# Two attention turns among the last gating slabs, tanh in the gate, first exponents in score banks, casts of the head norms in the second head

## What is computed

```python
p = softmax(q k^T)                       # 4 heads, 2 components each
a = p[:, :, 0] - lam * p[:, :, 1]
da = rmsnorm(a @ v, da_subln_w) * (1 - lam_init)
...
log_g = log_sigmoid(z @ w2 + b) / 16     # forward and backward gates
go = gla_bidirectional(gq / 8, gk, gv, log_g_f, log_g_b)
go = rmsnorm(go, gla_norm_w) * silu(gr)
h = h + concat([da, go]) @ w_out
```

## Time and profile before

| | us |
|---|---|
| median of 3 runs | 2437.65 |
| lowest, highest | 2434.55, 2437.88 |
| profiled execution | 2438.38 |
| its span in the profile | 2436.6 |
| granted TensorE clock, mean over the span | 0.984 |

### The profile page before, as it was taken

How to read it: one execution, slowest core, us unless ns; L and a number is a source line. 1 busy time by engine, 2 the same in 40 slices (tenths; PEclk the granted TensorE clock), 3 DMA queues, 4 the chain that set the end, 5 groups by cost and what they waited for, 6 DMA issues and landing times.

```text
span 2436.6 us, 38068 instructions
## 1 busy us (share of the span) xinstructions
PE 2334.8 (96%) x13568; PEld 1298.9 (53%) x13568; DVE 1700.0 (70%) x2984; ACT 1053.1 (43%) x1496; POOL 535.7 (22%) x418
## 2 busy tenths in 40 slices
PE   7999899999999998899999999988999989999998
PEld 3446774555555566655555555563444444443454
DVE  5326775578899989978888888868353447776235
ACT  4265442666666654543333333344422233332233
POOL 0001001567788631124222222104000010000001
PEclk9998999999999999999999999999999999999998
DMA  5200012487899669899999999913233323332321
GB/s 179 78 27 1 1 57 92 144 287 289 302 324 343 226 228 331 326 336 361 377 363 361 363 356 362 343 53 113 78 113 100 100 87 96 103 97 96 100 86 52
DMA packets 164871, 470.79 MB, mean 193 GB/s; under 512 B 17616, under 2 KB 70736, under 8 KB 163984
## 3 DMA queue, kind: packets, MB, share of 16 engines
q1 hardware_dynamic: 109312, 289.59, 34.9%
q0 software_dynamic: 36864, 134.23, 14.8%
q10 hardware_dynamic: 18576, 45.36, 4.9%
HBM read 421.67 MB, written 47.45 MB: 193 GB/s over the span
## 4 chain that ended last, share of the span: by engine, by line
PE 82%; DVE 12%; issue 2%; ACT 2%; DMA 1%; POOL 1%; DVEq 0%; SPq 0%; ACTq 0%; POOLq 0%
PE psum L536 25%; PE psum L537 24%; PE psum L538 24%; DVE arena L2043 2%; PE psum L426 1%; DVE arena L510 1%; DVE arena L2081 1%; DVE arena L2078 1%; DVE arena L2082 1%; PE psum L990 1%; PE psum L876 1%; PE psum L962 1%; DMA arena<-in_urows,arena 1%; PE psum L850 0%; DVE arena L2079 0%
## 5 line engine op out<-in xcount | busy, mean ns | idle before, releaser
L536 PE MATMUL psum<-arena 128*128 128x384 f16 (+2 forms) x3648 | 1261.3, 347 | 35.1 <-DVE arena L467 13.2
L537 PE MATMUL psum<-arena 128*128 128x384 f16 (+2 forms) x3648 | 1264.5, 347 | 0.0
L538 PE MATMUL psum<-arena 128*128 128x384 f16 (+2 forms) x3648 | 1257.7, 346 | 0.0
L536 PEld LDWEIGHTS psum<-arena 128*128 128x128 f16 x3648 | 354.2, 97 | 367.1 <-issue 51.2
L538 PEld LDWEIGHTS psum<-arena 128*128 128x128 f16 x3648 | 353.9, 97 | 324.0 <-issue 8.1
L537 PEld LDWEIGHTS psum<-arena 128*128 128x128 f16 x3648 | 353.6, 97 | 311.8 <-issue 8.1
L510 DVE SCALAR_TENSOR_TENSOR arena<-arena 128x1024 f16<-128x1024 f32 x216 | 268.2, 1244 | 297.6 <-ACT arena L497 297.1
L497 ACT ACTIVATE arena<-arena 128x1024 f16<-128x1024 f32 x216 | 226.1, 1050 | 255.9 <-PE psum L538 243.8
L1622 ACT ACTIVATE arena<-arena 128x1024 f16<-128x1024 f32 x128 | 135.3, 1057 | 299.8 <-PE psum L538 285.8
L516 POOL TENSOR_TENSOR arena<-arena 128x1024 f16<-128x1024 f32 x104 | 214.4, 2061 | 105.4 <-ACT arena L505 104.4
L438 POOL TENSOR_TENSOR arena<-arena 128x512 f32<-128x512 f32 x15 | 19.8, 1321 | 918.4 <-ACT arena L393 918.4
(11 more groups left out here) (251 smaller groups left out, 2179.7 us busy)
## 6 DMA issues: line engine op xcount, KB each, us to landing
arena<-in_w SPq DMA_DIRECT2D x320, 512.0 KB, 3.6
arena<-in_v SPq DMA_DIRECT2D x128, 512.0 KB, 6.0
early_activations<-arena ACTq DMA_DIRECT2D x124, 192.0 KB, 5.1
arena<-early_activations SPq DMA_DIRECT2D x124, 192.0 KB, 5.9
gate_matrix<-arena ACTq DMA_DIRECT2D x5, 4096.0 KB, 16.1
arena<-gate_matrix SPq DMA_DIRECT2D x32, 640.0 KB, 8.0
arena<-in_xT SPq DMA_DIRECT2D x4, 512.0 KB, 6.0
arena<-in_urows,arena POOLq DMA_INDIRECT x128, 6.9
```

Source lines behind the costliest of these rows:

```text
L536: nc.tensor.matmul(ps, a_h, b_h, start=first, stop=False)
L537: nc.tensor.matmul(ps, a_h, b_l, start=False, stop=False)
L538: return nc.tensor.matmul(ps, a_l, b_h, start=False, stop=last)
```

## The change

**Gating and the first two turns.** PE's scores of turn 0 stand between the second and the third gating slab, those of turn 1 between the third and the fourth. ACT's exponentials and DVE's maxima and differences of these turns follow the gate of the second and third slab in the same way. The first transposes wait for three gates, and the first mixing of values for the fourth. The gate is tanh(x/2) + 1 times x; its factor 1/2 and the slabs' scale are put into the recurrence's norm.

**Exponents 0 and 1** of the recurrence go to banks 1 and 3 instead of 6 and 7. Those of step 0 stand on PE ahead of turn 15's transposes, those of step 1 ahead of its values; ACT's exponentials move with them. The waits for the last transposes' copies and the last head's output pass to exponents 2 and 3. DVE's product of the meta keys moves behind the first level.

**Head norms.** In the first head DVE only scales; a new semaphore `head_scaled` releases the wide level. The casts and subtractions stand at the ends of the first eight steps of the second head.

```diff
         def expo(n, rows=P):
-            return psum[0:rows, (6 + n % 2) * 512:(7 + n % 2) * 512]
+            b = 6 + n % 2 if n >= 2 else 1 + 2 * n
+            return psum[0:rows, b * 512:(b + 1) * 512]
...
-            for n in range(N_GR, N_WO):
-                pe.wait_ge(gate_out, 1 + (n - N_GR + 1))
-                chunk(pe, n, slot(n), bank(4 + n - N_GR))
...
                 if turn == 0:
-                    pe.wait_ge(silu_out, HEADS)
+                    pe.wait_ge(silu_out, HEADS - 1)
...
             def mix_values(turn):
                 h, t = divmod(turn, TT)
                 pe.wait_ge(turn_out, turn + 1)
+                if turn == 0:
+                    pe.wait_ge(silu_out, HEADS)
...
-            pe.wait_ge(proj_out, 4)
-            for turn in range(HEADS * TT):
+            for n in range(N_GR, N_WO):
+                pe.wait_ge(gate_out, 1 + (n - N_GR + 1))
+                chunk(pe, n, slot(n), bank(4 + n - N_GR))
+                if n == N_GR + 1:
+                    pe.wait_ge(proj_out, 4)
+                    scores(0)
+                elif n == N_GR + 2:
+                    scores(1)
+            for turn in range(2, HEADS * TT):
                 scores(turn)
...
                 if n >= 2:
                     pe.wait_ge(e_exp, n - 1)
+                if n == 2:
+                    pe.wait_ge(turn_out, HEADS * TT)
+                elif n == 3:
+                    pe.wait_ge(av_out, HEADS)
...
                 if h == 0:
-                    pe.wait_ge(mixl_out, 1)
+                    pe.wait_ge(head_scaled, HEADS)
...
-                nc.scalar.activation(sgr[:, n - N_GR, :], bank(4 + n - N_GR), ACT.Sigmoid, scale=ISW).then_inc(sig_out, 1)
+                nc.scalar.activation(sgr[:, n - N_GR, :], bank(4 + n - N_GR), ACT.Tanh, scale=ISW / 2).then_inc(sig_out, 1)
+                if 1 <= n - N_GR <= 2:
+                    turn_exp(n - N_GR - 1)
...
+                nc.vector.scalar_tensor_tensor(out=sgr[:, n - N_GR, :], in0=sgr[:, n - N_GR, :], scalar=1.0,
+                                               in1=bank(4 + n - N_GR), op0=ALU.add,
+                                               op1=ALU.mult).then_inc(silu_out, 1)
+                if 1 <= n - N_GR <= 2:
+                    scores_max(n - N_GR - 1)
+                    difference(n - N_GR - 1)
...
+                scaled = nc.vector.scalar_tensor_tensor(out=o, in0=o, scalar=w, in1=bank(h),
+                                                        op0=ALU.mult, op1=ALU.mult)
+                if k == 0:
+                    scaled.then_inc(head_scaled, 1)
+                    return
+                dchain.link(scaled)
+                dchain.link(nc.vector.scalar_tensor_tensor(out=o, in0=o, scalar=ISW / 2, in1=sgr[:, h, :],
                                                            op0=ALU.mult, op1=ALU.mult))
-                if k:
-                    dchain.link(nc.vector.tensor_tensor(o, o, sgr[:, h, :], ALU.mult))
...
+            def head_cut(h, low):
+                o = otmp[:, h, :]
+                if not low:
+                    dve.wait_ge(head_scaled, h + 1)
+                    dchain.link(nc.vector.tensor_copy(xh[:, h, 0:T], o))
+                else:
+                    last = nc.vector.tensor_tensor(xl[:, h, 0:T], o, xh[:, h, 0:T], ALU.subtract)
+                    if h == HEADS - 1:
+                        last.then_inc(mixl_out, 1)
...
+                    if h == 1 and p < 2 * HEADS:
+                        head_cut(p // 2, p % 2)
```

More of the change, by code:

```diff
@@ L917, in _ @@
             pe.wait_ge(gate_cut, 1 + TT)
+            exponents(0)
+            turn_over(HEADS * TT - 1)
+            mix_values(HEADS * TT - 2)
             for h in range(HEADS):
@@ L1399, in _, with turn_exp @@
             last.then_inc(proj_out, 1)
+            def turn_exp(turn):
+                for c in range(2):
+                    u = 2 * turn + c
+                    act.wait_ge(max_done, u + 1)
+                    if turn >= 2:
+                        act.wait_ge(diff_done, turn - 1)
+                    nc.scalar.activation(pr[:, u % 4, :], psum[:, (2 * c + 1) * 512 - TM // 2:(2 * c + 1) * 512 + TM // 2], ACT.Exp,
+                                         bias=nmx[:, u % 4:u % 4 + 1],
+                                         accum_out=zs[:, u % 4:u % 4 + 1]).then_inc(exp_done, 1)
             cuts.upto(N_WO - 1)
@@ L1455, in step_exp @@
                                      scale=1.0 / (16 * GS)).then_inc(e_exp, 1)
+            turn_copy(HEADS * TT - 2)
             step_exp(0)
+            turn_copy(HEADS * TT - 1)
+            act.wait_ge(em_in, 1)
+            nc.scalar.activation(Emm[0:DH, :], bank(2, HEADS * M)[0:DH], ACT.Exp,
+                                 scale=1.0 / (16 * GS)).then_inc(em_exp, 1)
+            step_exp(1)
+            head_out(HEADS - 1)
             def head_squares(k, sqs, heads=range(HEADS)):
@@ L1847, in _ @@
             cuts.upto(N_WO - 1)
-            for n in range(N_GR, N_WO):
-                dve.wait_ge(sig_out, n - N_GR + 1)
-                nc.vector.scalar_tensor_tensor(out=sgr[:, n - N_GR, :], in0=bank(4 + n - N_GR), scalar=ISW,
-                                               in1=sgr[:, n - N_GR, :], op0=ALU.mult,
-                                               op1=ALU.mult).then_inc(silu_out, 1)
             def decayed(h, li):
```

58 lines of the change are left out of this document (20 added, 38 removed).

## The result

| | before | after |
|---|---|---|
| median of 4 runs, us | 2437.69 | 2421.30 |
| lowest, highest | 2434.55, 2437.88 | 2419.86, 2424.14 |
| profiled execution | 2438.38 | 2424.14 |
| its granted TensorE clock, mean | 0.984 | 0.989 |

Measured twice more, six runs each, the same kernel gave medians of 2425.39 and 2424.47; over all sixteen runs the median is 2424.1 (2419.86 to 2432.32), 13.4 us under 2437.5, the median of all 56 runs of the kernel before. The direction and the steps were right. What was wrong is the size of some terms, and how far one kernel's executions lie apart.

What follows compares the result with a forecast made beforehand. PE, busy for 96% of the span, was taken to bound the kernel. The terms 8.0 + 1.5 + 3.2 + 1.6 - 2.2 - 0.2 = 11.9 us gave 2425.8 us, range 2422.5 to 2432.5.

Steps and rivals of the forecast that it cites:

- part 1: Turns 0 and 1 between the gating slabs: turn 1's values mixed at 200.8 instead of 208.80, gain 8.0 us.
- part 2: Passage into the recurrence: first exponents in score banks remove PE's waits of 0.40 and 0.89 us, gain 1.5 us.
- part 3: Recurrence's first head: casts and subtractions moved out bring the wide level 3 x 1.07 = 3.2 us forward.
- the wide level at full clock: End of the recurrence's first head: PE's waits shrink and the clock stays at 2.4 GHz, another 1.6 us.
- casts in the second head: Recurrence's second head: moved casts and subtractions exceed DVE's idle time, loss 2.2 us, bounds 0 and 4.3.
- product with a scalar: Recurrence's norms: a product with a scalar replaces a plain one, 0.77 against 0.69 us, four times, loss 0.2 us.
- Rival D: Scores between slabs wait for a late key copy or exponential, and the slabs with them; 2428.5 us, chance 0.08.
- The sentence on the tanh: Gating slabs: tanh shares the exponentials' table and so allows the interleaving; the removed load by itself worth 0 to 0.1 us.
- All later stages only start earlier: Stages behind the edited stretch: assumed only to start earlier, with no further term added to the 11.9 us.
- A: Behind the slabs the clock falls again, holding back up to 6.8 us; gain 5.1, time 2432.5, chance 0.20.
- B: Ahead of the first head's wide level the clock still falls; gain 10.3, time 2427.4, chance 0.14.
- Rival C: Attention behind the slabs: half clock lasts over 24 us and the kernel is slower, 2441.8 at 32 us; chance 0.03.

Runs made afterwards that it cites:

- the version with the casts elsewhere: Changed kernel with the casts and subtractions four at a time in DVE's waits at the second step of the second and third heads; 2426.12 us, ratio 0.9949.
- the turns alone: Kernel before with only turns 0 and 1 between the gating slabs and the tanh gate; 2431.86 us, ratio 0.9984.
- the filling in the kernel before: Kernel before with ten matmuls that nobody reads in PE's two waits behind the slabs; 2433.64 us, ratio 0.9979.

## Why the prediction was right or wrong

All sizes below are from the first profile of after against that of before. PE stood 0.27 us earlier already at the gating slabs, ahead of anything the change touches, which is the start in the table; the lead at 400 us is 13.4 us.

| step | forecast, us | trace, us |
|---|---|---|
| start | 0 | 0.3 |
| part 1, turns among the slabs | 8.0 | 7.9 |
| part 2, exponents in score banks | 1.5 | 1.95 |
| part 3, up to the wide level | 3.2 | 3.6 |
| the wide level at full clock | 1.6 | 1.7 |
| casts in the second head | -2.2 | -2.0 |
| product with a scalar | -0.2 | 0.0 |
| sum | 11.9 | 13.4 |

**Part 1 was right, row by row.** Turn 2's scores at 192.65 (forecast 192.9), turn 3's 2.92 us later (2.9), turn 1's mixing 7.99 us after the slabs' end (7.9). Rival D did not occur: there is no idle time ahead of the third and fourth slab. Its timeline of DVE shows what was not foreseen, one line that took four times its usual time; the slab hid it, since the exponential after it was needed only behind the slabs:

```profile
186.10 2.12 DVE L1887 TENSOR_SCALAR arena<-arena 128x528 f32<-128x528 f32 x1
...
192.18 0.50 DVE L1887 TENSOR_SCALAR arena<-arena 128x528 f32<-128x528 f32 x1
```

**The sentence on the tanh was wrong.** "But it is what allows the interleaving" rested on no row. The right working would have been ACT's budget in a slab: 5.2 us against 0.6 for the gate, 1.4 for two exponentials and 2.6 for two loads. The tanh itself takes as long as the sigmoid, 1.09 us for two:

```profile
180.34 1.28 ACT L1421 ACT_TABLE_LOAD   x1
181.63 1.09 ACT L1421 ACTIVATE arena<-psum 128x512 f32<-128x512 f32 x2
184.20 0.70 ACT L1414 ACTIVATE arena<-psum,arena 128x528 f32<-128x528 f32 x1 [1.48 <-DVE arena L1877]
```

**Part 2 was 0.45 us too small.** The mis-sized term is PE's own work, which I had put at nothing. From the mixing of turn 1 to the first level before, the window is

```profile
208.80:258.97 50.17, 47.46 (x342) 36.27 (x340) 36.93 (x80) 31.98 (x84) 0.00 (x0) 1.00 0.00 1
```

with 50.17 - 47.46 = 2.71 us in which PE was not busy; after the change it is 48.22 - 46.93 = 1.29. So 1.4 us of idle time went: 0.40 + 0.89 are the two waits named, and a third of 0.14 us at 256.91 stands for the "some 0.2 us of shorter waits". The other 0.5 us is busy time, 47.46 against 46.93. By my reading the same matmuls overlap more where they follow one another without a stop: one of the exponents' matmuls takes 0.22 us, but the next starts 0.06 us after it (257.81 and 257.87 in before), so a stop behind one lays some 0.16 us bare. With two such stops and one behind a transpose gone, that makes most of the 0.5 us, an estimate from these rows.

**Part 3** brought the wide level 3.6 us forward instead of 3.2, since the distance from the first level to it went from 28.23 to 24.61 us. The mis-sized term is the 1.07 us of a step. The cast had to wait for the end of the scaling ahead of it, so the two stood 0.77 us apart; the products that now follow a scaling start after 0.65 us. The timelines of DVE, before and after, for the third scaling:

```profile
281.85 0.73 DVE L1904 SCALAR_TENSOR_TENSOR arena<-arena,psum 128x512 f32<-128x512 f32 x1
...
283.69 1.40 DVE L1863 TENSOR_TENSOR arena<-arena 64x512 f32<-64x512 f32 x2
```
```profile
270.50 0.74 DVE L1918 SCALAR_TENSOR_TENSOR arena<-arena,psum 128x512 f32<-128x512 f32 x1
271.15 1.40 DVE L1869 TENSOR_TENSOR arena<-arena 64x512 f32<-64x512 f32 x2
```

From scaling to product it was 1.84 us and is 0.65, so a step saves 1.19 us, and three of them 3.57. The loss in the second head was well placed and well sized: waits of 0.55, 0.81 and 0.46 us against one of 0.28 make 1.5 of the 2.0 us, and the version with the casts elsewhere takes back all of it.

**The product with a scalar costs nothing.** I took 0.77 us from a larger tile of 528 columns; on the 512 columns in question the row is the same as the 0.69 of the earlier trace rows:

```profile
361.39 0.69 DVE L1924 SCALAR_TENSOR_TENSOR arena<-arena 128x512 f32<-128x512 f32 x1
```

**What put the time outside the range** is the step "All later stages only start earlier", together with the treatment of the clock: the half-clock stretches of all the other code were taken over from the one profile of before, as if they belonged to the program. The terms above add 1.5 us to the forecast and alone would give 2424.3, inside the range, and next to the 2424.1 of sixteen runs. The other 3 us of the first measurement are luck: executions with fewer half-clock stretches. From 400 us on the two profiles of before have 53.6 and 43.3 us of them, the three of after 46.7, 50.3 and 46.9, in code that the change does not touch. Where PE is busy throughout, a stretch costs up to half its length (3.58 us against 1.90 at the wide level), so these 10 us are up to 5 us of time. The granted clocks of the runs without a profile say the same. The first four runs of the changed kernel average 0.9895, its twelve later ones 0.9881, which is 51 against 58 us at half clock in a run; half of the difference is 3.4 us, and the means of the times lie 3.7 us apart (2421.65 and 2425.38).

The runs shown before the prediction, 2434.55 to 2437.88, had been read as the scatter of this kernel; over 56 runs it was 2429.34 to 2444.88. A, B and the forecast had been given chances as if one of them were true of the program. They are outcomes of single executions, and the median mixes them. So is the row that had been set against A, the gap of 1.92 us at 281.23 without a fall: behind the same wait the clock did fall in the second profile of before (at 278.9), with the turns alone (273.4) and with the filling in the kernel before (276.0). A range made from all this would have reached some 3 us lower.

**Rival C** did not come in any run: the longest half stretch behind the slabs with the new order was 6.8 us.

Still open: why the clock falls in one execution and not in the next after the same waits, and how often it does, for which three profiles of a kernel are too few.

## What to carry to other kernels

Follow a change between landmarks on the bounding engine and price each distance apart; here six distances were right to 0.45 us while the end-to-end time of single executions moved by 12. Where PE's clock falls after short waits, treat the fall as something that happens in a share of the executions, take a second profile of the kernel before the forecast is made, and widen the range by the scatter of that clock over the whole kernel, not over the touched stretch. Before moved casts are put at step ends, look for the engine's longest wait: the same eight instructions cost 2.0 us at step ends and nothing in two waits. When an instruction is taken out of a chain, price the step from start to start, since what stood ahead of it may also be waited for less.

## What the runs showed of the hardware

- **A memset on POOL can hold up a DVE instruction.** The TENSOR_SCALAR of 0.50 us took 2.12 us beside six memsets, and ended 0.3 us after the last of them (timeline of POOL, changed kernel); it took 2.10 to 2.12 us in all eight profiles with the new slab order and the tanh:

```profile
185.09 2.84 POOL L2360 MEMSET arena<- 128x512 f32 x6
```

  In the version with the sigmoid the same two rows stand so:

```profile
184.85 0.73 DVE L1887 TENSOR_SCALAR arena<-arena 128x528 f32<-128x528 f32 x1
```
```profile
183.84 3.13 POOL L2360 MEMSET arena<- 128x512 f32 x6
```

  There the DVE instruction was 0.23 us late, and the memsets together took 0.29 us longer: by that it got in between two of them. The two-operand instruction behind it, beside the same memsets, kept its time (0.77 us), and so did two reductions beside an earlier memset of the changed kernel (1.32 us for both). This fits the exclusive lock on the port pair that DVE and GpSimd share, in the Trainium skill, "SBUF — State Buffer", section "SBUF: two separate sides": whoever starts first keeps it for a whole instruction. That memsets in a row can keep DVE out for longer than one of them is what this trace adds.
- **The clock.** It falls behind waits of 1.05 to 2.00 us in some executions and not in others, of the same program too, and in the stretches read here it stays low for 3.4 to 13.7 us.
- **Filling PE's waits can pay.** Ten matmuls that nobody reads made the kernel before 4.5 us faster, since they lie in waits behind which its clock fell in four of four profiles. In the new order, where it fell behind the slabs in three of six, thirteen of them showed no gain.
